# Clearing spread over the dense stage, in-place low parts in a six-deep ring, and the end of an expert reordered

## The reference

```
for layer in range(DEPTH):                       # DEPTH = 2
    shift, scale, gate = ada_modulation(c, w_mod_mix[layer], b_mod_mix[layer])
    h = normalize(x) * (1.0 + scale) + shift
    mix = token_mixer(h, ...)                    # w_in, attention a and c, pooling b, gates, branches, w_out
    x = layer_norm(ALPHA * x + (1.0 + gate) * mix, ...)
    ... the same modulation from w_mod_ffn ...
    y = swiglu(h, w1, w3, w2) if layer % 2 == 0 else moe_swiglu(h, w_router, b_router, w1, w3, w2)

def swiglu(h, w1, w3, w2):
    return (jax.nn.silu(h @ w1) * (h @ w3)) @ w2
# moe: per token the two largest router logits, softmax over the two,
#      y[token] += weight * swiglu(h[token]; expert)
```

## Time and profile before

| | |
|---|---|
| median of 3 runs | 1771.09 us (1769.48 to 1774.81) |
| profiled execution, its own time | 1762.26 us |
| its span | 1760.5 us |
| PE, DVE, ACT busy | 1648.9, 1357.8, 1022.7 us |
| bytes moved by DMA | 526.64 MB, mean 299 GB/s |
| granted clock of TensorE, mean | 0.98 |

### The profile page before, as it was taken

One profiled execution on the slowest core, in us unless ns is written; L12 is line 12 of the kernel. 1 busy time (PEld: TensorE's weight loads), 2 busy tenths in 40 slices (PEclk: granted clock), 3 DMA queues, 4 the chain that ended last, 5 costly groups with the idle time before them and its releaser, 6 DMA issues.

```text
span 1760.5 us, 20788 instructions
## 1 busy us (share of the span) xinstructions
PE 1648.9 (94%) x7272; PEld 1275.6 (72%) x7273; DVE 1357.8 (77%) x1147; ACT 1022.7 (58%) x824; POOL 69.7 (4%) x85
## 2 busy tenths in 40 slices
PE   6999897999999998999999989999899999999995
PEld 2587756888587765777877768888677777787773
DVE  5687765775797776889888886565588888888888
ACT  1375432334266433778777775545577877777773
POOL 1200030000100001000000000000000000000200
PEclk9999998999999998999999999999999999999998
DMA  9885459874496445999999996666699999999992
GB/s 365 308 317 186 144 190 394 320 273 148 166 341 220 148 168 192 394 396 371 393 374 356 395 384 226 215 221 213 217 369 388 375 395 395 391 388 341 389 393 109
DMA packets 217236, 526.64 MB, mean 299 GB/s; under 512 B 9889, under 2 KB 14161, under 8 KB 217185
## 3 DMA queue, kind: packets, MB, share of 16 engines
q1 hardware_dynamic: 208770, 496.15, 77.1%
q0 software_dynamic: 8336, 29.55, 4.6%
q10 hardware_dynamic: 80, 0.26, 0.0%
HBM read 518.85 MB, written 15.47 MB: 304 GB/s over the span
## 4 chain that ended last, share of the span: by engine, by line
PE 78%; DVE 10%; issue 5%; DMA 3%; ACT 2%; ACTq 0%; DVEq 0%; SPq 0%
PE ps L1535 19%; PE ps L1537 19%; PE ps L1536 18%; PE ps L1541 5%; PE ps L1542 4%; DVE w_lo L1391 4%; PE ps L1546 4%; DMA w_raw<-in_ffn_w_dram 2%; PE ps L2036 2%; PE ps L2067 1%; DMA w_raw<-in_w_mod_mix_dram 1%; PE ps L1576 1%; ACT w_hi L814 1%; DVE gates L1170 1%; DMA w_raw<-in_w_in_dram 1%
## 5 line engine op out<-in xcount | busy, mean ns | idle before, releaser
L1391 DVE TENSOR_TENSOR w_lo<-w_raw,w_hi 128x2048 fp32r<-128x2048 f32 x333 | 756.5, 2288 | 173.4 <-ACT w_hi L814 171.1
L814 ACT CAST w_hi<-w_raw 128x2048 fp32r<-128x2048 f32 x333 | 633.6, 1910 | 178.9 <-PE ps L1542 86.9
L1535 PE MATMUL ps<-w_hi,actT_hi 128*128 128x512 f32 (+1 forms) x1464 | 583.2, 398 | 48.0 <-DVE w_lo L1391 17.3
L1537 PE MATMUL ps<-w_hi,actT_lo 128*128 128x512 f32 (+1 forms) x1464 | 569.0, 389 | 0.0
L1536 PE MATMUL ps<-w_lo,actT_hi 128*128 128x512 f32 (+1 forms) x1464 | 568.3, 388 | 0.0
L1535 PEld LDWEIGHTS ps<-w_hi,actT_hi 128*128 128x128 f32 x1464 | 278.1, 190 | 123.7 <-issue 35.0
L1537 PEld LDWEIGHTS ps<-w_hi,actT_lo 128*128 128x128 f32 x1464 | 277.8, 190 | 57.6
L1536 PEld LDWEIGHTS ps<-w_lo,actT_hi 128*128 128x128 f32 x1464 | 278.6, 190 | 53.9 <-issue 1.7
L954 DVE TENSOR_TENSOR w_lo<-w_raw,w_hi 128x2048 fp32r<-128x2048 f32 x81 | 185.4, 2289 | 104.0 <-ACT w_hi L551 103.7
L551 ACT CAST w_hi<-w_raw 128x2048 fp32r<-128x2048 f32 x81 | 154.5, 1908 | 132.4 <-PE ps L1537 91.9
L1541 PE MATMUL ps<-w_hi,gT_hi 128*128 128x512 f32 x448 | 182.3, 407 | 8.6 <-DVE gT_hi L1418 5.4
(11 more groups left out here) (281 smaller groups left out, 1204.7 us busy)
## 6 DMA issues: line engine op xcount, KB each, us to landing
w_raw<-in_exp_w_dram SPq DMA_DIRECT2D x336, 1024.0 KB, 7.6
w_raw<-in_ffn_w_dram SPq DMA_DIRECT2D x33, 1024.0 KB, 5.4
w_raw<-in_w_mod_mix_dram SPq DMA_DIRECT2D x24, 1024.0 KB, 11.4
w_raw<-in_w_mod_ffn_dram SPq DMA_DIRECT2D x24, 1024.0 KB, 5.7
w_raw<-in_w_gate_dram SPq DMA_DIRECT2D x24, 1024.0 KB, 6.7
w_raw<-in_w_in_dram SPq DMA_DIRECT2D x14, 1024.0 KB, 6.4
w_raw<-in_w_out_dram SPq DMA_DIRECT2D x8, 1024.0 KB, 5.1
by_row<-constants_dram POOLq DMA_DIRECT2D x16, 512.0 KB, 18.4
```

Source lines behind the costliest of these rows:

```text
L814: nc.scalar.copy(w_hi[:, i % SPLIT, :], w_raw[:, i % RING, :]).then_inc(split_hi, 1)
L1391: TTn(w_lo[:, i % SPLIT, :], w_raw[:, i % RING, :], w_hi[:, i % SPLIT, :].bitcast(F32), ALU.subtract).then_inc(piece_used, 1)
L1535: MM(to, hi, w_h, start=first, stop=False)
L1537: return MM(to, lo, w_h, start=False, stop=last)
```

## The change

1. **Clearing.** Each of the 16 copies of zeros waits on `split_used`: the first until PE has multiplied 3 pieces of the dense stage, the n-th (from 0) until it has multiplied 3 + 3n//2. 
2. **Ring.** `SPLIT` is 6. `w_lo` has six slots and lies at the address of `w_raw`: DVE subtracts in place. `w_hi` has six slots, so the buffers take the same 12 pieces of memory. A slot is free for the next load only when PE has multiplied its piece, so SP's loads wait on `split_used`; only after a "mod" piece they wait on `piece_used`. Slots run on from stage to stage (`first_slot`). ACT and DVE split the next expert's pieces 0 to 3 before the expert begins (0 to 2 before).
3. **Turns with one tile.** The gated values are turned into bank 6 (`turned_bank`), at once after the first A piece of the next panel. The next expert's rows are turned behind the last gated panel, into banks 2 and 3 (`TURN_FREE`), and are signalled in two halves, so that the first piece waits for one half only. 
4. **Count.** PE loads the next expert's count behind these turns, and copies a register at the loop's head.

Cut to its core (the rest renames indices):

```diff
-RING, SPLIT = 6, 3
+RING, SPLIT = 6, 6
+UNSPLIT = 3
+LAG = 3
+LATE = 3
...
+    def slot(self, i):
+        return (self.first_slot + i) % RING
...
+def turned_bank(blocks, b):
+    return HW1 + 2 if blocks == 1 else HW1 + 2 * b
...
-TURN_EARLY, TURN_LATE = (6, 7), (5, 7)
+TURN_FREE, TURN_LATE = (2, 3), (5, 7)
...
+        w_hi = sb("w_hi", [P, SPLIT, PIECE], F32R)
+        in_place = ExitStack()
+        w_lo = sb("w_lo", [P, RING, PIECE], F32R, scope=in_place)
+        in_place.close()
         w_raw = sb("w_raw", [P, RING, PIECE])
-        w_hi = sb("w_hi", [P, SPLIT, PIECE], F32R)
-        w_lo = sb("w_lo", [P, SPLIT, PIECE], F32R)
...
@@ SP, stream of loads @@
-                    if i < RING:
-                        sp.wait_ge(piece_used, base + i + 1 + (gap if i < RING // 2 else 0))
-                    elif i < RING + stretch.raw:
-                        sp.wait_ge(split_used, split_base + i - RING + 1 + SPLIT)
+                    old = before.pieces[before.n - RING + i] if i < RING else stretch.pieces[i - RING]
+                    if old[0] == "mod":
+                        sp.wait_ge(piece_used, base + i + 1 - (0 if i < RING else stretch.raw))
+                    elif i < RING:
+                        sp.wait_ge(split_used, split_base + before.split_no[before.n - RING + i] - before.n_split + 1 + SPLIT)
                     else:
-                        sp.wait_ge(piece_used, base + i + 1 - stretch.raw)
-                    load(i % RING, piece, mod_layer if piece[0] == "mod" else layer, expert)
+                        sp.wait_ge(split_used, split_base + stretch.split_no[i - RING] + 1 + SPLIT)
+                    load(stretch.slot(i), piece, mod_layer if piece[0] == "mod" else layer, expert)
...
@@ POOL @@
                     for n in range(EXPERTS * TT):
+                        gp.wait_ge(split_used, MIX.n_split + 3 + 3 * n // 2 + SPLIT)
                         gp.dma_start(by_row[n * P:(n + 1) * P, :], consts[:, C_ZERO:C_ZERO + D]).then_inc(rows_cleared, 16)
...
@@ ACT, expert, one panel @@
-                                round_at(7, loads, done)
+                                if blocks == 1:
+                                    gT_part(at)
+                                round_at(8, loads, done)
                                 gate_of(5, done, at, folds)
-                                round_at(8, loads, done)
-                                gT_part(at)
                                 round_at(9, loads, done)
+                                if blocks == 2:
+                                    gT_part(at)
+                                round_at(10, loads, done)
...
-                                for i in (10, 11, 12):
+                                for i in (11, 12, 13):
                                     round_at(i, loads, done)
...
@@ DVE, expert, tail @@
                                 gT_part(panel_0 + NP)
-                                rest_at(11, done6)
                                 if last:
                                     copy_sums(False)
                                     return
                                 rest_at(12, done6)
-                                turned_rows(0, e + 2, TURN_LATE if blocks == 2 else TURN_EARLY)
+                                turned_rows(0, e + 2, TURN_LATE if blocks == 2 else TURN_FREE)
                                 rest_at(13, done6)
                                 rest_at(14, done6)
                                 copy_sums(packed or few)
+                                rest_at(15, done6)
...
@@ PE, expert @@
+                    next_count = nc.alloc_registers("next_count", engines=[pe.engine])
+                    nc.regs_mov(next_count, pe.value_load(counts_i[0:1, 0:1], min_val=0, max_val=SEQ))
                     stay_busy(2, 3)
                     with nc.Fori(0, EXPERTS, engines=[pe.engine], hint_back_edge=True) as e:
-                        count = pe.value_load(counts_i[0:1, bass.ds(e, 1)], min_val=0, max_val=SEQ)
+                        count = nc.snap(next_count, min_val=0, max_val=SEQ)
...
-                                up(4, "A", 0, done)
+                                up(4, "A", 0, done, turn_previous if blocks == 1 else None)
                                 up(5, "A", 1, done)
                                 pe.wait_ge(gated_ready, at)
-                                up(6, "B", 0, done, turn_previous)
+                                up(6, "B", 0, done, turn_previous if blocks == 2 else None)
...
-                            if blocks == 1:
-                                with pe.If(e < EXPERTS - 1):
-                                    turn_rows(0, e + 1, TURN_EARLY)
-                                turn(panel_0 + NP)
-                                with pe.If(e > EXPERTS - 2):
-                                    turn_places()
...
+                            turn(panel_0 + NP)
+                            with pe.If(e < EXPERTS - 1):
+                                turn_rows(0, e + 1, TURN_FREE if blocks == 1 else TURN_LATE)
+                                nc.regs_mov(next_count, pe.value_load(counts_i[0:1, bass.ds(e + 1, 1)], min_val=0, max_val=SEQ))
+                            with pe.Else():
+                                turn_places()
```

More of the change, by code:

```diff
@@ L149, in __init__ @@
         for i, piece in enumerate(pieces):
-            landed[i % RING] += 32 if piece[0] == "branch" and piece[2] == 0 else 16
-            self.loads.append(landed[i % RING])
+            landed[self.slot(i)] += 32 if piece[0] == "branch" and piece[2] == 0 else 16
+            self.loads.append(landed[self.slot(i)])
             self.split_no.append(None if piece[0] == "mod" else n)
@@ L440, in _ @@
             for layer in range(DEPTH):
-                stream(MIX, layer * LAYER_PIECES + MOD0.n_used, layer, mod_layer=("ffn", layer), gap=layer * (RING // 2),
-                       split_base=layer * LAYER_SPLITS)
+                stream(MIX, layer * LAYER_PIECES + MOD0.n_used, layer, DENSE if layer else MOD0, layer * LAYER_SPLITS, mod_layer=("ffn", layer))
                 if layer < 1:
-                    stream(DENSE, MOD0.n_used + MIX.n_used, 0, mod_layer=("mix", 1), gap=RING // 2, split_base=MIX.n_split)
+                    stream(DENSE, MOD0.n_used + MIX.n_used, 0, MIX, MIX.n_split, mod_layer=("mix", 1))
                 else:
                     moe0 = MOD0.n_used + LAYER_PIECES + MIX.n_used
-                    sp.wait_ge(piece_used, moe0 + RING)
+                    assert [piece[0] for piece in MIX.pieces[-RING:]] == ["mod"] + ["branch"] + ["out"] * (RING - 2)
+                    sp.wait_ge(piece_used, moe0 - (RING - 1) + RING)
                     with sp.Fori(0, EXPERTS) as e:
-                        stream(EXPERT, e * EXPERT.n + moe0, 1, expert=e)
+                        stream(EXPERT, None, 1, EXPERT, e * EXPERT.n_split + LAYER_SPLITS + MIX.n_split, expert=e)
             for t in range(TT):
@@ L548, in round_piece @@
                 j = stretch.split_no[i]
-                act.wait_ge(raw_loaded[i % RING], load_base[i % RING] + stretch.loads[i])
-                act.wait_ge(split_used, split_base + j + 1 - (stretch.raw if j < 2 * SPLIT else 0))
-                nc.scalar.copy(w_hi[:, j % SPLIT, :], w_raw[:, i % RING, :]).then_inc(split_hi, 1)
+                slot = stretch.slot(i)
+                act.wait_ge(raw_loaded[slot], load_base[slot] + stretch.loads[i])
+                act.wait_ge(split_used, split_base + j + 1 - (stretch.raw if j < stretch.raw + SPLIT else 0))
+                nc.scalar.copy(w_hi[:, (j - stretch.raw) % SPLIT, :], w_raw[:, slot, :]).then_inc(split_hi, 1)
             def stream(stretch, load_base, split_base, after):
                 for i, piece in enumerate(stretch.pieces):
-                    if piece[0] == "mod" or i < SPLIT:
+                    if piece[0] == "mod" or i < UNSPLIT:
                         continue
                     j = stretch.split_no[i]
-                    after(j - SPLIT)
+                    after(j - LAG)
                     round_piece(stretch, i, load_base, split_base)
-                for j in range(stretch.n_split - SPLIT, stretch.n_split):
+                for j in range(stretch.n_split - LAG, stretch.n_split):
                     after(j)
@@ L1775, in _ @@
                 second_tile(layer * 2, 0)
-                for i in range(SPLIT):
+                for i in range(UNSPLIT):
                     project_raw(i, 1).then_inc(split_used, 1)
                 for i, piece in enumerate(MIX.pieces):
-                    if piece[0] == "mod" or i < SPLIT:
+                    if piece[0] == "mod" or i < UNSPLIT:
                         continue
@@ L1897, in swiglu @@
                     second_tile(1, 4)
-                    for i in range(SPLIT):
+                    for i in range(UNSPLIT):
                         up_raw(i, 1).then_inc(split_used, 1)
                     for i, (kind, p, *rest) in enumerate(stretch.pieces):
```

(2 more changed lines are left out.)

205 lines of the change are left out of this document (107 added, 98 removed).

## The result

The changed kernel takes 1759.82 us (median of 5 runs, 1756.8 to 1763.68), the kernel before 1771.09 (1766.64 to 1774.81): ratio 0.9939, 95% interval [0.9917, 0.9962], 11.3 us faster, with 7 to 15 as the interval. Forecast were 29.6 us and 1742.

A forecast was written before the change was run, and what follows sets the result against it. PE, stalled by loads behind copies of zeros, bounded the dense stage; two or three things nearly at once held few-row experts, PE the second and seventh. 14.6 + 0 + 13.8 + 1.2 = 29.6 off 1771.09: about 1742, range 1716 to 1764.

The forecast's parts named there:

- rival B: Experts gain nothing, being DMA-bound already, with gaps from later issues; only the clearing counts: 1756.5 us; chance 0.20.
- D: Rival: spread copies of zeros cost as much as bunched ones, while the experts gain: 1756 us; chance 0.06.
- the prediction's own sign: Wrong if the experts together change by under 5 or over 30 us, or the dense stage keeps over 3 of its gap.
- A limit of slots: Few-row panels: three `w_hi` slots make ACT wait for PE before rounding; the change lifts this limit. Panel 16.33 us.
- Clearing, -14.6: Dense stage: spreading the copies of zeros removes PE's stall near 280 to 304 us; -14.6 us, bounds 0 and -16.
- Ring in panels, -13.8: 30 few-row panels go from 16.33 us to the DMA's 15.9, some experts gaining more; -13.8 us, bounds 0 and -35.
- the play: Few-row expert behind a slower one: the refilled ring lets it run at PE's pace until 3.0 us are gone; -4.2 us.
- Rival A: DMA is not the cap: PE sets few-row panels, over 400 GB/s; 1721 us, or 1713 with ends; chance 0.12.
- the slot's cycle: Few-row panels: landing 5.0, rounding 1.91, splitting 2.29, PE 2.75, semaphores 0.2 make 12.2 of 15.2 us, leaving 3.0.
- Turns, halves and count move work at the experts' ends only: PE-bound second and seventh experts: nothing changes inside them, where PE does 17.09 us a panel with no wait.
- rival C: Slower: slots stay taken until PE has multiplied; landing at 10.3 us makes panels 17.45 us, in all 1790; chance 0.07.
- Ends and count, -0.6 for each PE-bound expert: Second and seventh experts: half of the head's 1.45 us wait for `actT_lo` goes; -1.2 us together, bounds +2 and -5.

The follow-up runs named there:

- half_before: The kernel before with only half of each expert's weights loaded, every engine instruction keeping its size; 1767.04 us, 0.9984.
- round_three: The changed kernel, but in the experts' heads and panels ACT rounds only when PE is through with the third piece before; 1809.26 us, 1.022.
- clear_turn: The kernel before plus the spread clearing and the gated values' turn behind the first A piece; ring and DVE's head order as before; 1745.71 us, 0.9863.
- turn_old: The changed kernel with the panel's turn back in its old place, between the two B pieces; 1765.41 us, 0.9988.
- clear_only: The kernel before with nothing but the 16 waits of the copies of zeros added; 1753.21 us, 0.9912.
- half_after: The changed kernel with only half of each expert's weights loaded, every engine instruction keeping its size; 1725.0 us, 0.9744.
- gate_first: The changed kernel, but at a one-tile expert's head DVE computes panel 0's gated values ahead of the splits of pieces 5 and 6; 1755.4 us, 0.991.
- hold_entry: The changed kernel, but the first expert's loads of pieces 6 and on wait until DVE has split its piece 4; 1763.01 us, 0.9959.
- dve_three: The changed kernel, but DVE splits an expert's piece 3 at the loop's head again, not ahead of the loop; 1751.15 us, 0.9904.
- pad32: The changed kernel with 32 semaphore instructions added at the start of DVE's code, where it waits for data; 1757.76 us, 0.9938.
- three_gate: The changed kernel with both dve_three's and gate_first's moves; 1744.69 us, 0.9871.

## Why the prediction was wrong

The ledger lacks 24.2 us of the 29.6: 13.0 between the dense stage and the first expert's piece 5, 6.7 in the heads, and 6.6 in the few-row panels and ends together; the other experts gave 2.1 more than forecast. The measured 1759.8 lies in the stated range, 1716 to 1764, but that is luck: the range reached so far up for rivals B and D, and neither is what happened. By the prediction's own sign (the experts together change by less than 5 us) it was wrong too: from piece 5 on they changed by 3.7.

**What bounds the kernel** was read right for the dense stage. For few-row panels it was half right. That DVE's and ACT's rates and the DMA's were not the limit is shown (half_before: 16.35 us at 193 GB/s). "A limit of slots" is refuted as it stood: with the same limit of three the panel is 16.00 (round_three) or 16.05 (clear_turn) once the turn stands behind the first A piece. The ring and the turn's place together make it: the turn without the ring gives 5.6 of the 12.4 us in these panels (clear_turn), the ring without the turn none (turn_old). I cost the turn's move at nothing inside a panel.

**Clearing, -14.6**: right. The stall itself is 14.6 us shorter, the dense stage ends 13.2 us earlier, and alone it gives 0.9912 of 1771.09, 15.6 us, with 11 to 20 as the interval (clear_only). Its working was too light in one place: with a "mod" piece to every two split ones, 1.5 pieces of PE work stand beside 2.25 loads and not 1.5, 7.3 us of DMA in 8.3. The slack hid the copies all the same: the DMA's share is 0.88 in the window above.

**Ring in panels, -13.8**: the size was nearly right, 12.4 us in the few-row panels of the profiled pair, and so was the rule: two panels at PE's 15.1 behind a slower expert, then the DMA's 15.95. The parts were not: the play spent (what five panels take less than 5 x 15.96) was 0.4 us in the third expert and 1.4 to 1.9 in the first and fifth, not 3.0, and the sixth expert gained 3.6 where 1.2 was forecast. Its long head of 21.4 us gave the loads time to run ahead, which no run tests by itself; so the sum came near in part by luck. The cap, 15.9 at 394 GB/s, is shown by half_after. Rival A is thereby refuted: 412 GB/s at the start of the program is not reached here.

**The first step that failed is "it may spend the play"**, the slot's cycle of 12.2 us against 15.2, together with "Turns, halves and count move work at the experts' ends only". The cycle took the landing at 5.0 us; it was 8.2, with which the same sum is 15.4 us and leaves no play against PE's 15.1. And I added it up for a panel and used it for the whole expert. At a one-tile expert's head the chain also holds two loads of ACT's tables (1.28 us each), silu, a second rounding, two splits and the gated values, 18 us as shown above. The heads I had put at nothing cost 6.7 us. Of the 18 us it is the order in the queues that costs, not the load: the wait stays with half the bytes (1.95 us, half_after), it goes when DVE computes the gated values two splits earlier (gate_first), and it isn't there when the turn is early but DVE's place for the gated values the old one (clear_turn). The few-row ends cost 5.2 more: pieces that land just in time are split late, and DVE's small steps for which PE waits queue behind them, as at the last expert's last turn:

```profile
1722.46 0.66 PE L2069 MATMUL ps<-cst,gated 128*128 128x128 f32 x4 [1.01 <-DVE gated L1430]
...
1725.38 0.79 PE L1569 MATMUL ps<-w_hi,gT_hi 128*128 128x512 f32 x1 [2.04 <-DVE gT_hi L1443]
```

That the loads' pace makes the ends long is shown by half_after (14.9 to 15.0 us instead of 17.0). In clear_turn, with the ring and the end's order of before, they are 15.8 us; which of these two does it was not tried. As far as it is the ring, it is rival C's mechanism, slots held too long for the DMA's pace, at the ends and not in the panels. The time of rival B came out nearly (1756.5), but not its reason: the panels did gain.

**The second step that failed, and the larger, is the sum itself**: that 14.6 us won in the dense stage are still won at the end. 12.6 of them are left where the mixer before the experts ends, 10.3 when DVE reaches `pick_w` (it now splits piece 3 before that, 2.3 us), and 0.4 at its first split in the loop, because DVE stands 17.9 us at the entry instead of 8.0. PE's lead of 18.4 us at piece 0 ends in its wait of 13.84 for piece 4. I had named such a stand, of PE, and written that the change leaves it; that rested on where it comes alone, and it is 4.45 us now, where it was 7.18. Of DVE's I had costed none. Each of its three steps stands behind a branch (7.5, 4.0 and 4.9 us), and with the loads held back (hold_entry) they were 0.7, 2.8 and 0.6 us shorter, of which the first lies within what other kernels show (6.6 to 7.5). What DVE waits for in them no row names, and so their cause is not shown. The first, of 7.5 us at the loop's start, is gone when DVE doesn't split piece 3 ahead of the loop (dve_three, where 1.2 and 6.0 us remain behind the inner branches). Why is open: it isn't the count of instructions in front by itself (pad32), nor the bytes under way (7.3 us in half_after). Other shifts than 32 were not tried.

**Ends and count, -0.6 for each PE-bound expert**: the size came once the head was mended (122.1 in gate_first, 122.7 before); the end itself gained 1.2. Its cause is not shown: clear_turn has 122.1 and 122.2 without the new order at the end and without the count's move.

## What to carry over

A move is costed for each place where the loop's order is broken: its head, its end, its first pass. Of a ring whose slots are held longer, walk once around the ring at the head, through every instruction in the queues on the way, not only in the steady state. When one engine asks for a value earlier, look whether the engine that makes it has it earlier in its own queue, and not later, as here. And before an early gain is added to a sum, ask who takes part at the next meeting point and whether he can be there earlier: here DVE couldn't. Two versions beat the changed kernel by 12 to 14 us: clear_turn (1745.71) and three_gate (1744.69), which differ by less than their intervals. The first reaches it without the long ring.

## What the runs showed of the hardware

In 80 us of few-row panels, with whole expert loads at work, the DMA queues moved 395 GB/s in the kernel before (957 to 1037 us), 392 in the changed kernel (717 to 797) and 395 in clear_turn (1400 to 1480), while the median from issue to landing was 8.8, 8.2 and 7.0 us; in turn_old they moved 384 (1400 to 1480), at 7.4 us. In the two-tile expert of the kernel before (1100 to 1200 us), with 21 loads in 100 us at 221 GB/s, it was 5.0. DVE's stands behind its three branches at the entry to the loop, with the same work behind them, ranged over the sixteen kernels from 0.5 or less to 7.5 us, from 1.2 to 4.1 and from 2.2 to 6.0. With the loads held back (hold_entry) the second fell from 4.0 to 1.2 us; with half the bytes (half_after) it stayed at 3.8.
